# Sparse heads' value products with the values as weights in two column halves, head outputs copied first in a slot, and five search steps moved into attention

## The reference, cut to what matters

```
h  = rms_norm(x) * (1 + sc1) + sh1
z  = h @ w_in                                   # queries, keys, values, indexer
# 4 differential heads of 128:
a  = softmax(q1 k1 + bias) - lam * softmax(q2 k2 + bias)
od = rms_norm(a @ v, g_subln) * (1 - lam_init)
# 8 sparse heads of 64, 2 key/value heads:
score = sum_h w[h] * relu(qi[h] . ki)           # indexer
sel   = top_k(score, 256)                       # 80 for the new tokens
os    = softmax(q k[sel] + bias) @ v[sel]
m  = concat(od, os) @ w_out
x  = x + ga1 * rms_norm(m)
x  = x + ga2 * rms_norm(swiglu(rms_norm(x) * (1 + sc2) + sh2))
```

## Time and profile before

| what | value |
|---|---|
| median of 3 runs | 1751.34 us |
| the profiled execution | 1766.02 us, span 1764.3 us |
| PE busy | 1610.8 us (91%) |
| DVE, ACT, POOL busy | 731.7, 547.1, 393.1 us |
| chain that ended last | PE 73%, DVE 16%, issue 3%, ACT 3%, DMA 3% |
| search on DVE | from 190.5 to 425.8 us |
| attention's slots | from 428.2 us to about 897 us |
| FFN groups | from 952.1 us to the end |

### The profile page before, as it was taken

The page is one execution under the profiler, slowest core; times in us unless marked ns, Lnnn a source line. Parts: engine busy times, 40 slices in busy tenths (PEclk is TensorE's granted clock), DMA queues, the critical chain, the costliest instruction groups (busy, mean ns, idle before and its releaser), DMA issues.

```text
span 1764.3 us, 24074 instructions
## 1 busy us (share of the span) xinstructions
PE 1610.8 (91%) x9035; PEld 1345.6 (76%) x9055; DVE 731.7 (41%) x1751; ACT 547.1 (31%) x1134; POOL 393.1 (22%) x335
## 2 busy tenths in 40 slices
PE   5699999992899889999986999999999999999996
PEld 2586889991455566565645999999999999999995
DVE  0613899998455554544435113032131221312205
ACT  1745322211455554454535111121211112211112
POOL 0511111110111111000127313223232232231214
PEclk9999999995699999999987999999999999999998
DMA  8310456523434433342153111111011110201006
GB/s 264 96 43 25 122 183 191 182 74 108 149 103 114 115 109 90 104 109 74 34 156 102 57 36 48 48 48 48 24 50 45 48 48 24 71 24 48 0 1 119
DMA packets 148568, 146.95 MB, mean 83 GB/s; under 512 B 12125, under 2 KB 129182, under 8 KB 148490
## 3 DMA queue, kind: packets, MB, share of 16 engines
q1 hardware_dynamic: 147258, 141.46, 27.3%
q0 software_dynamic: 1232, 4.46, 1.4%
HBM read 126.60 MB, written 19.29 MB: 83 GB/s over the span
## 4 chain that ended last, share of the span: by engine, by line
PE 73%; DVE 16%; issue 3%; ACT 3%; DMA 3%; POOL 1%; SPq 1%; POOLq 0%; DVEq 0%; ACTq 0%
PE S L1909 30%; DVE scrap L1309 11%; PE T L1924 10%; PE PJ L1830 7%; PE PJ L1924 5%; PE PJ L1872 5%; PE PJ L1668 5%; PE S L1770 4%; PE T L1748 3%; DMA ada_more<-in_w_ada 1%; PE S L1687 1%; DVE sc L1478 1%; PE S L1777 1%; ACT aT L1099 1%; PE T L1853 1%
## 5 line engine op out<-in xcount | busy, mean ns | idle before, releaser
L1909 PE MATMUL S<-h2h,gh 128*128 128x352 f32 (+1 forms) x1056 | 347.1, 329 | 2.0 <-DVE top L1555 2.0
L1909 PE MATMUL S<-h2h,gl 128*128 128x352 f32 (+1 forms) x1056 | 346.3, 328 | 0.0
L1909 PE MATMUL S<-h2l,gh 128*128 128x352 f32 (+1 forms) x1056 | 346.2, 328 | 0.0
L1580 DVE TENSOR_TENSOR hv<-sg,S 128x352 f32<-128x352 f32 (+1 forms) x66 | 35.1, 532 | 497.5 <-ACT sg L1222 497.5
L1909 PEld LDWEIGHTS S<-h2h,gh 128*128 128x128 f32 x1056 | 199.2, 189 | 2.5 <-issue 2.2
L1909 PEld LDWEIGHTS S<-h2l,gh 128*128 128x128 f32 x1056 | 199.9, 189 | 0.4
L1909 PEld LDWEIGHTS S<-h2h,gl 128*128 128x128 f32 x1056 | 199.1, 189 | 0.0
L1309 DVE TENSOR_SCALAR_CACHE_REDUCE scrap<-work,cand 128x384 uint8<-128x384 f32 (+6 forms) x217 | 177.9, 884 | 1.1
L1668 PE MATMUL PJ<-hTh,wh 128*128 128x352 f32 (+3 forms) x504 | 169.0, 335 | 0.0
L1668 PE MATMUL PJ<-hTl,wh 128*128 128x352 f32 (+3 forms) x504 | 166.3, 330 | 0.0
L1668 PE MATMUL PJ<-hTh,wl 128*128 128x352 f32 (+3 forms) x504 | 166.2, 330 | 0.0
(11 more groups left out here) (205 smaller groups left out, 2455.7 us busy)
## 6 DMA issues: line engine op xcount, KB each, us to landing
graw<-in_w_gu SPq DMA_DIRECT2D x44, 512.0 KB, 5.0
ada<-in_w_ada SPq DMA_DIRECT2D x20, 1024.0 KB, 7.6
draw<-in_w_down SPq DMA_DIRECT2D x22, 512.0 KB, 3.3
wraw<-in_w_in SPq DMA_DIRECT2D x20, 512.0 KB, 5.8
q_scratch<-qst SPq DMA_DIRECT2D x8, 544.0 KB, 2.9
xin<-in_x_p SPq DMA_DIRECT2D x8, 512.0 KB, 3.7
ada_more<-in_w_ada SPq DMA_DIRECT2D x4, 1024.0 KB, 12.5
xt<-in_x_p SPq DMA_DIRECT2D x8, 512.0 KB, 5.1
```

Of the source, the lines that this page charges most:

```text
L1909: last = pe.matmul(S[u % 2][:, 512 * part:512 * part + n], wp[:, slot, k, 128 * part:128 * part + 128], hp[:, k, c0:c0 + n], start=(k == 0 ...
```

## The change

It has three parts.

1. The search is cut: `PROJ_STEPS = 28` steps stay in front of attention, and the parts of the last five (seven counts and one update each, 40 parts) are spread over three points in each of the slots 0 to 12. A moved count writes `scrap2` (it lies over `eq`, which is used only after that) and every one of them is linked.
2. Sparse heads: DVE scales the probabilities themselves by the reciprocal (in slot s+1, 2 instructions over all keys), so PE's transposes wait for `scaled` and no longer for `exp_done`. The product has 64 columns of values as weights and the transposed probabilities (up to 128 columns) moving, m = 0 into partitions 0 to 63 and m = 1 into partitions 64 to 127 of `PJ[0]`, key block by key block in turn. The result is already transposed, so ACT copies it straight to `oT` (`pair_out`), and DVE's two reads, PE's transpose and a bank of `T` fall away for these heads.
3. ACT copies head outputs earlier in a slot: `pair_out` first of all, `head_out` after the probability copies and before the two exponentials.

```diff
+PROJ_STEPS = 28
+LATE_PARTS = [(j, i) for j in range(PROJ_STEPS, STEPS) for i in range(len(TOPK_TILES) + 1)]
+LATE_POINTS = 3 * 13
+def late_parts(slot, point):
+    at = 3 * slot + point
+    if at >= LATE_POINTS:
+        return []
+    return LATE_PARTS[len(LATE_PARTS) * at // LATE_POINTS:len(LATE_PARTS) * (at + 1) // LATE_POINTS]
...
-    if _s >= 3:
+    if _s >= 3 and not sparse(_s - 3):
         T_ORDER += [("o", _s - 3)]
...
+            def pair_out(s):
+                t, i, r, _ = step(s)
+                act.wait_ge(pv_done, s + 1)
+                act_copy(oT[:, t % 2, i, 0:r], PJ[0][:, 0:r]).then_inc(o_read, 1)
...
             for slot in range(SLOTS):
+                if 3 <= slot < NSTEPS + 3 and sparse(slot - 3):
+                    pair_out(slot - 3)
                 for part in range(2):
                     for key in prob_part(slot, part):
                         prob_out(*key[1:])
                 t = tie_stage(slot, 1)
                 if t:
                     equals_out(t)
+                if 3 <= slot < NSTEPS + 3 and not sparse(slot - 3):
+                    head_out(slot - 3)
                 if slot < NSTEPS:
                     ...
-                if 3 <= slot < NSTEPS + 3:
-                    head_out(slot - 3)
...
+                out = scrap[0:r, o:o + n] if j < PROJ_STEPS else scrap2[0:r, 0:n]
+                ins = nc.vector.tensor_scalar(out, work[0:r, o:o + n], least_score, None, ALU.is_ge, ALU.add,
+                                              accum_out=rows_at(count, i))
+                if t == TOPK_TILES[-1] or j >= PROJ_STEPS:
+                    link(ins)
...
-            for j in range(STEPS):
-                search_step(j)
+            for j in range(PROJ_STEPS):
+                for i in range(len(TOPK_TILES) + 1):
+                    search_part(j, i)
...
+                    if 1 <= slot <= NSTEPS and sparse(slot - 1):
+                        s = slot - 1
+                        _, _, r, n = step(s)
+                        p = sc[0:r, s % 3, m, 0:n]
+                        nc.vector.tensor_scalar(p, p, rinv[0:r, s % 4, m:m + 1], None, ALU.mult
+                                                ).then_inc(scaled, 1)
+                    for part in late_parts(slot, m):
+                        search_part(*part)
-                if 2 <= slot < NSTEPS + 2:
+                if 2 <= slot < NSTEPS + 2 and not sparse(slot - 2):
...
                     dve.wait_ge(pv_done, s + 1)
...
-                    if sparse(s):
-                        for m in range(2):
-                            last = nc.vector.tensor_scalar(ob[0:r, s % 2, 64 * m:64 * m + 64],
-                                                           PJ[0][0:r, 64 * m:64 * m + 64],
-                                                           rinv[0:r, s % 4, m:m + 1], None, ALU.mult)
-                        last.then_inc(o_read, 1)
...
                     gated(t)
+                for part in late_parts(slot, 2):
+                    search_part(*part)
...
                 if sparse(s):
-                    pe.wait_ge(exp_done, 2 * s + m + 1)
+                    pe.wait_ge(scaled, scaled_count(s, m))
...
-                    for m in range(2 if sparse(s) else 1):
-                        out = PJ[0][0:r, 64 * m:64 * m + 64] if sparse(s) else PJ[0][0:r, 0:128]
-                        c, e = (512 + 64 * ((i - 4) // 2), 64) if sparse(s) else (128 * i, 128)
-                        for j, (o, w) in enumerate(blocks):
-                            vt_ = j if t < 8 else 8 + j
-                            last = pe.matmul(out, aT[0:w, m, j, 0:r], vsb[0:w, vt_, c:c + e],
-                                             start=(j == 0), stop=(j == len(blocks) - 1))
+                    for j, (o, w) in enumerate(blocks):
+                        vt_ = j if t < 8 else 8 + j
+                        edge = dict(start=(j == 0), stop=(j == len(blocks) - 1))
+                        if sparse(s):
+                            c = 512 + 64 * ((i - 4) // 2)
+                            for m in range(2):
+                                last = pe.matmul(PJ[0][64 * m:64 * m + 64, 0:r], vsb[0:w, vt_, c:c + 64],
+                                                 aT[0:w, m, j, 0:r], **edge)
+                        else:
+                            last = pe.matmul(PJ[0][0:r, 0:128], aT[0:w, 0, j, 0:r],
+                                             vsb[0:w, vt_, 128 * i:128 * i + 128], **edge)
                     last.then_inc(pv_done, 1)
```

More of the change, by code:

```diff
@@ L310, in build @@
         eq = then("eq", [128, 1024], BF16)
+        eq_end = base[0]
+        scrap2 = place("scrap2", [128, 1024], mybir.dt.uint8, eq_end - 2048)
+        base[0] = eq_end
         eqT = then("eqT", [128, 8, 128], BF16)
@@ L1122, in head_out @@
                     act.wait_ge(m_done, 2 * (t - 1))
-                gain = {} if sparse(s) else {"scale": subln[:, 0:1]}
-                act_copy(oT[:, t % 2, i, 0:r], bank[:, 0:r], **gain).then_inc(freed(("o", s)), 1)
+                act_copy(oT[:, t % 2, i, 0:r], bank[:, 0:r], scale=subln[:, 0:1]).then_inc(freed(("o", s)), 1)
             def out_out(t, half):
@@ L1303, in rows_at, with counted, search_part, search_update @@
                 return tile[0:rows_of(TOPK_TILES[i]), i:i + 1]
[L1305 to L1316, removed]
+            def counted(j, i, least_score):
+                t = TOPK_TILES[i]
+                r, n, o = rows_of(t), nkeys(t), WORK0[t]
+                out = scrap[0:r, o:o + n] if j < PROJ_STEPS else scrap2[0:r, 0:n]
[4 more added lines that the diff above has]
+                else:
+                    ins.then_inc(vchain, 1)
+                    chain[0] += 1
+            def search_part(j, i):
+                if i == len(TOPK_TILES):
+                    search_update(j)
+                else:
+                    counted(j, i, 0.0 if j == 0 else TINY if j == 1 else rows_at(cand, i))
+            def search_update(j):
                 if j == 0:
-                    dve.wait_ge(targets_set, 3 * len(TOPK_TILES) + 1)
-                    counted(lambda i: 0.0)
                     link(nc.vector.tensor_tensor(good[:, :], count[:, :], target[:, 0, :], ALU.is_ge))
@@ L1494, in _ @@
                     dve.wait_ge(pv_done, s + 1)
[L1495 removed]
+                    if i >= 2:
                         t_wait_full(dve, ("o", s - 2))
[L1497 to L1512 removed]
+                    elif t:
+                        t_wait_full(dve, ("o", s - 6))
+                    nc.vector.tensor_scalar(ob[0:r, s % 2, :], PJ[0][0:r, 0:128], rinv[0:r, s % 4, 0:1], -1.0,
+                                            ALU.mult, ALU.mult).then_inc(o_read, 1)
+                    dve.wait_ge(o_read, s + 1)
+                    if diff_count(s) > 1:
+                        dve.wait_ge(o_squared, diff_count(s) - 1)
+                    nc.vector.tensor_tensor_reduce(out=obj[0:r, :], in0=ob[0:r, s % 2, :],
+                                                   in1=ob[0:r, s % 2, :], scale=1.0, scalar=0.0, op0=ALU.mult,
+                                                   op1=ALU.add, accum_out=oss[0:r, s % 2:s % 2 + 1]
+                                                   ).then_inc(o_squared, 1)
                 t = tile_at(slot, 15)
@@ L1822, in out_projection @@
                     pe.wait_ge(rank_read, rank_count(t + 1, 1))
-                for i in range(8 * t, 8 * t + 8):
+                for i in range(8 * t, 8 * t + 4):
                     t_wait_freed(pe, ("o", i))
+                pe.wait_ge(o_read, 8 * t + 8)
                 out_products(t, half, range(KB // 2))
@@ L1843, in _ @@
                     turn_equals(tie_stage(slot, 1))
-                if 3 <= slot < NSTEPS + 3:
+                if 3 <= slot < NSTEPS + 3 and not sparse(slot - 3):
                     s = slot - 3
                     r = rows_of(s // 8)
[L1848 to L1851, removed]
+                    pe.wait_ge(o_ready, diff_count(s))
                     bank = t_wait_free(pe, ("o", s))
```

8 lines of the change are left out of this document (5 added, 3 removed).

## The result

The changed kernel takes 1709.22 us in the median of four runs (1707.01 to 1710.38), against 1751.8 us in four runs of the kernel before: ratio 0.9736, 95% interval 0.9682 to 0.9789. The forecast was 1702 us, in a range of 1690 to 1732. The kernel before scatters: 19 further executions have a median of 1761.77 us (1750.82 to 1764.57). The changed kernel stays within 4 us. How far TensorE's clock explains that is taken up with the experiments.

The account below looks back on a forecast made before the run. The search alone bounds attention's start, no engine fills slots 0 to 10, PE bounds from 477.5 us. Terms -10.2 - 23.9 - 0.9 - 7.9 - 5 - 1 = -48.9 us, from median 1751.34 to 1702 us; range 1690 to 1732.

Parts of the forecast that it names:

- Term 1: Attention's start: five search steps moved into slots 0 to 12; slot 0 23.6 us earlier, partly paid back, -10.2 us.
- The rival of the fully exposed search: Slots 0 to 12: all 36.5 us of moved search lie on the loop, +12.9 us, 1725 us; chance 0.12.
- Terms 2 and 3: Attention on PE: sparse products with halves side by side, -23.9 us; transposes of `ob` dropped, -0.9 us.
- the half of tiles 1 and 2: Sparse products: half the saving in these tiles dropped because tile 1's slots aren't PE's alone; 25.2 became 23.9 us.
- the rival of slots that don't follow: Slots without output projection: half of what PE is spared turns into waits, 1720 us; chance 0.18.
- The rival of the serial halves: Sparse products: the two halves take turns, so the product's saving becomes +5.5 us, 1732 us; chance 0.08.
- the slower case: Sparse products: halves take turns with each weight load between them, 31 us in all, 1763 us; chance 0.05.
- Term 4: Attention from 477.5 us: PE's waits for the copy to `oT` go, -7.9 us; fewer half-clock windows, -5 us.
- The clock's part: Half-clock windows between 477.5 and 897 us: fewer of them, -5 us, bounds +12 and -12.
- Term 5: DVE and ACT in sparse slots: at most 0.93 us more scaling, covered; last head's way through `T` goes, -1 us.

Follow-up runs that it names:

- the pairs alone: Changed kernel with all 33 search steps ahead of attention and differential head copies behind the exponentials, leaving the sparse heads' new product, scaling and direct copy: 1716.71 us.
- The last experiment: Changed kernel with three search steps moved, spread over slots 0 to 10 only, and differential head copies behind both exponentials: 1706.72 us.
- the copies alone: Kernel before with only ACT's copy of every head output moved ahead of the two exponentials: 1749.12 us, ratio 0.994.

## Why the prediction was right, and where it was not

The profiled executions are 1766.02 and 1709.16 us. What the terms were worth between them is taken up first, and the number 1702 last.

**Term 1 (-10.2 us by slot 11; measured -11 to -12, and -8 to -11 by slot 13).** The start came as worked out: slot 0 is 24.0 us earlier where 23.6 were forecast. Slots 0 to 10 took 49.15 us where 50 were forecast: the moved work is 44.1 - 17.1 = 27.0 us of busy DVE there and not 30.9, and DVE is idle for 5.1 us and not 2. About 3 of these 5.1 us are waits for another engine, and some 2 are the short gaps between linked instructions, which the forecast had in its 30.9. So the two sizes were off by about 2 and 1 us the opposite ways. What failed is the cover of slots 11 and 12. I had the output projection hide 2.81 us in each. Slot 12 took 4.99 us before, at full clock; in the changed kernel it takes 6.44 us, at full clock too, of which DVE is busy 6.06; with the pairs alone slots 11 and 12 took

```profile
461.80:472.90 11.10, 10.93 (x39) 5.79 (x39) 4.83 (x23) 4.11 (x13) 1.48 (x4) 0.91 0.19 40
```

and in the two executions of the changed kernel 13.0 and 14.5 us, at a mean clock of 0.89 and 0.80. The last experiment has 12.3 us at 0.82 with DVE out of the way. At like clocks (0.89 against 0.91, 0.80 against 0.82) about 2 us are given back to DVE, inside the bound of 5.6 but not the nothing that the sum has. The 1.5 us between the two executions is the clock, which comes back during slot 11. The timeline of slot 12 shows the order of it: the combination, then moved work ahead of the second bias instruction, then more of it ahead of DVE's read of the product.

```profile
460.18 0.49 DVE L1520 SCALAR_TENSOR_TENSOR sc<-sc,rlam 128x256 f32<-128x256 f32 x1
460.58 1.14 DVE L1338 TENSOR_SCALAR_CACHE_REDUCE scrap<-work,cand 128x896 uint8<-128x896 f32 x1
461.77 0.42 DVE L1511 CUSTOM_DVE_ANT_0 sc<-S,ering 128x256 f32<-128x256 f32 x1
462.12 1.28 DVE L1338 TENSOR_SCALAR_CACHE_REDUCE scrap<-work,cand 128x1024 uint8<-128x1024 f32 x1
463.44 0.35 DVE L1541 TENSOR_SCALAR ob<-PJ,rinv 128x128 f32<-128x128 f32 x1
```

The rival of the fully exposed search is refuted: it had slot 11 at 12.9 us later than before.

**Terms 2 and 3 (-24.8 us; measured about -27).** The halves run at once, 1.68 us for 28 records where 1.57 plus 0.22 were forecast. From the first execution of the kernel before to the second of the changed one slots 13 to 71 lose 46.0 us. 10.0 of them are 23.9 us of half clock at 0.42, and 9.0 the waits for `oT` as the copies alone showed them; 27 us remain for products, transposes and new waits.

PE's own time divides them further. In the changed kernel's second execution it is

```profile
465.40:834.93 369.53, 339.70 (x2106) 200.12 (x2106) 218.83 (x587) 204.36 (x486) 48.63 (x93) 1.00 0.37 103
```

so PE is busy 42.0 us less and idle only 4.0 us less than in the kernel before, though 9.5 us of waits went: others of about 5.5 us came, the 11.3 us before the sparse products among them. Some 10 of the 42 are the clock, the other 32 products and transposes. The sum had the products of tiles 1 to 7 about right, 25.2 us before the half of tiles 1 and 2 was dropped, where their durations fell by 27. Tile 8 it had wrong: it took that as nothing, and there twelve records took 1.23 to 1.26 us before and 0.64 after.

Sparse slots without output projection did follow: slot (6, 7) went from 8.88 us to 6.69, more than its product saves, and with that the rival of slots that don't follow is refuted. In tiles 1 and 2 the half that I dropped was rightly dropped: slots (2, 0) and (3, 0) are even 0.4 us longer, and the four slots with each tile's sparse products are shorter by 0.6 and 0.8 us together. The rival of the serial halves, and with it the slower case, is refuted by six records under way at once, and by what the kernel with the halves one after the other loses.

By the Trainium skill (TensorE: Matmul & The Clock Gate, Part 3) weight loads overlap running products only when their row groups differ. The trace doesn't agree: the halves share all rows, and in the 1.68 us of the product PE is busy throughout while its weight loads are busy for 1.50 us.

```profile
715.68:717.36 1.68, 1.68 (x28) 1.50 (x28) 1.00 0.78 239
```

**Term 4 (-7.9 and -5 us; measured -9 and -10).** The waits went, but the credit was half misplaced. I had written that differential heads are copied before the exponentials, as if that were needed; in the changed kernel it brings nothing that shows, as the new pairs alone already remove the waits. The clock's part was named with bounds of 12 on both sides and came out at the lucky end in this pair of executions: the 23.9 us of half clock fell to 0 in one and to 6.8 in the other. Which part of the new pairs keeps the clock up isn't shown; the copies alone left 10.2 us.

**Term 5 and the added wait.** DVE's work from slot 13 on rose from 202.25 to 218.92 us and is covered, as forecast. PE's wait for `scaled` shows as 2.5 us in all.

**The base of the sum.** That 1709 came out so near 1702 is partly luck. Each term was worked out on an execution of 1766.02 us, which gave 1717; the changed kernel's profiled execution took 1709.16, so the terms together were 8 us too small. I then took all 48.9 us from a median of 1751.34 that came from three executions, 14.7 us lower, and this was the larger error, the other way. The clock's part can't be had from an execution that has little half clock to begin with, and the executions near 1751 have less: their mean granted clock was 0.961 to 0.965, that of the profiled one 0.956. Against the median of 19 executions, 1761.77, the gain is 52.6 us and the sum of terms 4 us too small; against the first four, 42.6 us, it is 6 us too large.

## What to carry to other kernels

A product with few moving columns and full-width weights can cost as much as one with twice the columns: here 0.112 us a record with 64 and with 128 moving. Taking the narrow operand as weights, two halves side by side, cut it from 3.15 to 1.68 us, and three quarters of that need the halves to alternate in the program (2.80 us otherwise). Before moving work into gaps of a pipeline, check the slot in which the clock is already back: the room there is smaller than the slots around it suggest, and how much to move is found by trying sizes, not by filling the gap (three steps beat five by 6 us). When a kernel's runs scatter by 1%, profile it twice before a change is credited or charged with a few microseconds of clock.

## What the runs showed of the hardware that I had not expected

- Products of two column halves run at once, full-height weights and loads included: 28 records in 1.68 us when the halves alternate. If all of one half's are listed first, only the records around the change of half overlap: 2.80 us.
- The clock's half-speed windows are mostly a matter of the single execution: one program had 30.7 and 41.0 us of them in the same 58 slots, and each microsecond cost 0.42 us (about 0.5 by the 33 executions of the kernel before). In the kernels with the new pairs they fell to 0 to 6.8 us, and the spread of the changed kernel's executions was 4 us where it had been 16; with the copies alone it was 10.2 us of half clock and a spread of 13.
